# A hybrid decoder trunk on eight cores: attention moved off two PSUM banks, wider masks, a second set of group buffers in the first mixer

## The chip, the cores and the metric

The program runs on all 8 cores of one Trainium2 chip. Each core does one sequence of the batch of 8 alone; nothing is exchanged. The metric is device time in microseconds of the slowest core, the median of several runs. The profile is of one execution, read on its slowest core (core 4).

## The reference

Two layers over x of 8 x 2048 x 1024 (one core: 2048 x 1024). Cut to what matters:

```python
x = x + mamba2_mixer(rms_norm(x, a_norm), ...)        # 8 groups of 4 heads: in_proj, width-4 conv, SSD scan, gated norm, out_proj
x = x + conv_ffn(x, ...)                              # layer 0
k, v = split(rms_norm(x, kv_norm) @ w_kv + b_kv); k = rotary(rms_norm(k, k_norm), positions)
q = rotary(rms_norm(rms_norm(x, b_norm) @ w_q + b_q, q_norm), positions)
x = x + sliding_window_sink_attention(q, k, v, sinks) @ w_o + b_o   # window 128, 16 q heads, 4 kv heads
x = x + conv_ffn(x, ...)                              # layer 1

def sliding_window_sink_attention(q, k, v, sinks):
    # blocks of 128 queries against their own and the previous block of 128 keys
    scores = einsum("bnqhgd,bnkhd->bnhgqk", qb, k_band) * d ** -0.5
    mask = (rel >= 0) & (rel < WINDOW) & (kpos >= 0)
    probs = softmax(concatenate([where(mask, scores, -inf), sink], -1))[..., :-1]
    return einsum("bnhgqk,bnkhd->bnqhgd", probs, v_band)

def conv_ffn(x, norm_g, w_in, conv_w, conv_b, w_down):
    gate, val = split(rms_norm(x, norm_g) @ w_in, [2816])
    return (silu(causal_dwconv(gate, conv_w, conv_b)) * val) @ w_down
```

## The kernel before

The 2048 tokens are cut into four blocks (b = 0 to 3) of 512. The work is written as lists of steps: `mixer_steps(b)`, `mixer_out(b)`, `ffn_steps(b, l)`, `attn_steps(b)`. `weave` merges lists by their costs. In order: mixer 0 alone, its output projection alone; then for b = 0, 1, 2 a stretch with the feed-forward layers beside mixer b + 1, and a stretch with attention of block b beside the output projection of block b + 1; then the last block. In the trace (its page and windows) mixer 0 takes the first 240 us, the three attention stretches lie at about 550 to 650, 1050 to 1155 and 1550 to 1640 us, attention of block 3 lies beside a feed-forward layer near 1800 to 1960 us.

The order in which each engine takes instructions is not that of the lists. Every operation is recorded with a cost and its dependences (`_deps_for`: a PSUM bank is one unit), and `schedule` plays the program: each engine takes the ready operation with the lowest number. So an engine's queue is fixed when the program is built, and at run time a queue stands still when its next instruction waits.

PSUM has 8 banks. Mixers 1 to 3 use banks 0 and 1 for the input projection (`b_in`), 2 for everything small (`b_x`), 3 for the scan's output (`yb`). Their first steps are four norms (transposes `sb_cm,sb_Cs`), then `dt1`: 8 matmuls with 96 output partitions (`sb_hM,sb_ring_mw`, 96x512), a chain of activations and vector operations, and matmuls `sb_cf,sb_Ssb`, `sb_cf,sb_Eb` (`toks`). Attention of blocks 0 to 2 takes its banks from `fh`: projections 1 to 7 in turn, scores the pairs (2,3) and (4,5) in turn, 6 for the output and 7 for the denominators, 1 for `wo` (the output weights, `sb_ring_fw,sb_uF`). The block's output projection (`mixer_out`, `sb_ring_mw,sb_ybuf`) has bank 0 alone. The 34 uses of the projection banks end with `rot(9)` (`sb_fln,sb_cm`, then DVE operations), which falls on bank 6.

Attention is cut into units, one for a pair of kv heads, 128 queries and 128 keys: 14 in block 0, 16 in each other, 62 in all. `qk(u)` issues two 64-row score matmuls (`sb_hF,sb_kT`) and two 32-row matmuls that add the mask as a product of two constants (`sb_cm`); ACT takes the exponential of both banks; `pv(u)` issues two pairs of 64-column matmuls (`sb_facc,sb_vtok` and `sb_facc,sb_cm`). After two units `norm` runs on DVE and ACT before the banks 6 and 7 are free again. Matmuls recorded with `mmg` (line 362 of the profile), `mm` (349) and `tr` (367) carry these names.

A step `yst(t)` of the scan issues two `mmg` groups of four 64-column matmuls. All mixers keep one set of group buffers (`macc`, `Er`, `Eb`, `Wt`, `Cs`, `xtok`, `xE`, `Btok`, `CBb` and others); `fetch(g)` loads `Er` through the SP queue.

## Time and profile before

| | |
|---|---|
| time, median of 3 runs | 2098.79 us (2096.45 to 2115.26) |
| the profiled execution, its own time | 2089.89 us |
| its span on the slowest core (cores: 2070.2 to 2088.8) | 2088.8 us |
| PE busy | 1880.0 us, 90% |
| DVE busy | 1403.8 us, 67% |
| ACT busy | 1328.4 us, 64% |
| chain that ended last | PE 77%, DMA 8%, DVE 5%, ACT 5%, issue 5% |

The span is the time from the first to the last instruction on one core; the device time of that execution is 1.1 us more. TensorE (PE) is busy nine tenths of it, so the question of any change is what it does to the missing tenth, to the clock, and to how closely matmuls follow each other. In the timeline rows the first number is the start, the second how long the piece lasts; a bracket at the end is the idle time before it and who ended it.

### The profile page before, as it was taken

What the parts mean: (1) busy time and instruction counts of PE and PEld (TensorE: products, weight loads), DVE (VectorE), ACT (ScalarE), POOL (GpSimd) and SP (SyncE); (2) the same over time, 40 slices, a digit from 0 to 9 for tenths busy, and PEclk for the clock granted to TensorE, in tenths of its full rate; (3) what the DMA queues carried; (4) which work ended last, traced back from release to release, by engine and by line L of the source; (5) the groups of instructions that cost most, each with busy time, mean ns of one, the idle gap of its engine ahead of it and who ended that gap; (6) DMA issues with size and microseconds to landing.
All of it is one profiled execution on the core that took longest, in us unless ns stands there. A gap on an engine that the chain in (4) does not pass through costs nothing.

```text
span 2088.8 us, 34694 instructions; the slowest of 8 cores (2070.2 to 2088.8 us)
## 1 busy us (share of the span) xinstructions
PE 1880.0 (90%) x10024; PEld 837.9 (40%) x10024; DVE 1403.8 (67%) x2404; ACT 1328.4 (64%) x2238; POOL 203.8 (10%) x325
## 2 busy tenths in 40 slices
PE   4777789998897999999888899999988799999999
PEld 2333344444433444444432444444443344433344
DVE  5687578887745866678674776688675465683462
ACT  4688567978756566666656766677565543675430
POOL 0122101122111011000120000001102000020000
PEclk9999889999899999999999899999989899999999
DMA  8899669898638999845331454644412344333344
GB/s 201 174 213 217 161 148 212 206 220 203 171 102 179 204 220 223 253 141 169 112 121 59 123 162 161 205 151 148 142 61 92 108 154 137 122 131 107 112 154 153
DMA packets 111065, 330.58 MB, mean 158 GB/s; under 512 B 14752, under 2 KB 33312, under 8 KB 110880
## 3 DMA queue, kind: packets, MB, share of 16 engines
q1 hardware_dynamic: 95184, 271.53, 39.9%
q0 software_dynamic: 15696, 56.83, 17.8%
q8 instruction: 86, 1.41, 0.3%
q14 instruction: 99, 0.81, 0.1%
HBM read 318.74 MB, written 66.39 MB: 184 GB/s over the span
## 4 chain that ended last, share of the span: by engine, by line
PE 77%; DMA 8%; DVE 5%; ACT 5%; issue 5%; SPq 0%; DVEq 0%; POOL 0%; ACTq 0%; POOLq 0%
PE ps_ps L349 69%; PE ps_ps L362 6%; DMA sb_ring_mw<-w 3%; PE ps_ps L367 2%; DMA w<-sb_ring_fw 1%; DMA sb_Er<-er_scr 1%; DMA sb_ring_fw<-w 1%; DVE sb_macc L401 1%; ACT sb_facc L385 1%; DVE sb_hF L390 1%; DMA sb_xR<-x 1%; ACT sb_fsq L385 1%; DVE sb_xR L390 0%; ACT L385 0%; ACT sb_Cs L385 0%
## 5 line engine op out<-in xcount | busy, mean ns | idle before, releaser
L349 PE MATMUL ps_ps<-sb_hF,sb_ring_fw 128*128 128x512 bf16 x2464 | 579.9, 385 | 9.9 <-DVE sb_hF L390 6.3
L349 PE MATMUL ps_ps<-sb_hM,sb_ring_mw 128*128 128x512 bf16 (+1 forms) x1568 | 399.8, 394 | 34.7 <-DVE sb_macc L401 25.7
L349 PE MATMUL ps_ps<-sb_ring_fw,sb_uF 128*128 128x512 bf16 (+1 forms) x1696 | 397.8, 381 | 11.2 <-DVE sb_hF L390 3.6
L349 PEld LDWEIGHTS ps_ps<-sb_hF,sb_ring_fw 128*128 128x128 bf16 x2464 | 239.0, 99 | 295.3 <-issue 37.0
L401 DVE SCALAR_TENSOR_TENSOR sb_macc<-ps_ps,sb_cst,sb_macc 128x511 f32<-128x511 f32 (+2 forms) x384 | 282.2, 744 | 12.5 <-PE ps_ps L349 1.4
L385 ACT ACT_TABLE_LOAD x194 | 248.9, 1283 | 43.3 <-PE ps_ps L362 15.5
L401 DVE SCALAR_TENSOR_TENSOR sb_facc<-ps_ps,sb_cst,sb_facc 128x511 f32<-128x511 f32 x352 | 261.6, 745 | 17.5 <-PE ps_ps L349 2.9
L349 PEld LDWEIGHTS ps_ps<-sb_ring_fw,sb_uF 128*128 128x128 bf16 x1696 | 160.5, 99 | 203.4 <-issue 41.6
L349 PEld LDWEIGHTS ps_ps<-sb_hM,sb_ring_mw 128*128 128x128 bf16 (+1 forms) x1568 | 151.3, 101 | 218.7 <-issue 70.6
L385 ACT ACTIVATE sb_facc<-ps_ps,sb_cst 128x512 f32<-128x512 f32 x197 | 150.1, 763 | 135.7 <-PE ps_ps L349 120.0
L390 DVE TENSOR_TENSOR sb_xR<-sb_xR,ps_ps 128x512 f32<-128x512 f32 x128 | 86.8, 685 | 170.3 <-PE ps_ps L349 161.4
L349 PE MATMUL ps_ps<-sb_ring_mw,sb_ybuf 128*128 128x512 bf16 (+1 forms) x608 | 156.3, 389 | 15.4 <-DVE sb_ybuf L401 8.1
L385 ACT ACTIVATE sb_macc<-ps_ps,sb_cst 128x512 f32<-128x512 f32 x135 | 103.8, 769 | 76.0 <-PE ps_ps L349 71.4
L385 ACT ACTIVATE sb_uF<-sb_facc 128x512 bf16<-128x512 f32 x176 | 109.7, 628 | 58.1 <-DVE sb_facc L401 54.4
L390 POOL TENSOR_TENSOR sb_stmp<-sb_prevF,sb_cdec 128x256 f32<-128x256 f32 x128 | 83.9, 655 | 620.0 <-DVE sb_prevF L390 425.5
L390 DVE TENSOR_TENSOR sb_uF<-sb_uF,ps_ps 128x512 bf16<-128x512 bf16 x176 | 119.7, 681 | 31.6 <-PE ps_ps L349 30.2
L385 ACT ACTIVATE sb_prevB<-sb_prevF 128x256 bf16<-128x256 f32 x128 | 52.6, 411 | 74.2 <-PE ps_ps L349 30.8
L390 DVE TENSOR_TENSOR sb_facc<-sb_facc,sb_fix_f 128x2 f32<-128x2 f32 x176 | 29.8, 169 | 97.8 <-ACT sb_halo_f L385 91.3
L349 PEld LDWEIGHTS ps_ps<-sb_ring_mw,sb_ybuf 128*128 128x128 bf16 x608 | 56.5, 100 | 92.1 <-issue 41.9
L390 DVE TENSOR_TENSOR sb_prevF<-sb_stmp,ps_ps 128x256 f32<-128x256 f32 x128 | 53.3, 416 | 54.3 <-PE ps_ps L349 41.1
L401 DVE SCALAR_TENSOR_TENSOR sb_ytmp<-sb_xcb,sb_cst,ps_ps 128x256 f32<-128x256 bf16 x128 | 56.8, 476 | 37.0 <-PE ps_ps L362 36.8
L413 POOL DMA_DIRECT2D sb_ring_fw<-w x76 | 41.8, 550 | 392.4 <-PE ps_ps L349 352.5
(200 smaller groups left out, 2325.6 us busy)
## 6 DMA issues: line engine op xcount, KB each, us to landing
sb_ring_fw<-w SPq DMA_DIRECT2D x218, 512.0 KB, 3.8
sb_ring_mw<-w SPq DMA_DIRECT2D x106, 512.0 KB, 5.0
sb_ring_fw<-w POOLq DMA_DIRECT2D x76, 512.0 KB, 9.6
w<-sb_ring_fw SPq DMA_DIRECT2D x76, 512.0 KB, 8.3
sb_ring_mw<-w POOLq DMA_DIRECT2D x32, 512.0 KB, 9.5
w<-sb_ring_mw SPq DMA_DIRECT2D x32, 512.0 KB, 7.7
sb_Er<-er_scr SPq DMA_DIRECT2D x32, 512.0 KB, 7.6
sb_xR<-x SPq DMA_DIRECT2D x16, 512.0 KB, 9.2
```

Source lines behind the costliest of these rows:

```text
L349: return self.add("pe", lambda e: e.matmul(out, lhsT, rhs, start=start, stop=stop), [lhsT, rhs] + ([] if start else [out]), [out], cost=ma ...
L362: ins = e.matmul(out, lhsT, rhs, start=start, stop=stop)
L367: return self.add("pe", lambda e: e.transpose(out, in_, ident), [in_, ident], [out], cost=250.0 if _f32(in_) else 80.0)
L385: return self.add("act", lambda e: e.activation(out, in_, func, **kw), rd, wr, cost=c, tab=TABLE.get(func, 0))
L390: return self.add(eng, lambda e: e.tensor_tensor(out, in0, in1, op), [in0, in1], [out], cost=c)
L401: return self.add("dve", lambda e: e.scalar_tensor_tensor(out, in0, scalar, in1, op0, op1), rd, [out], cost=190.0 + 1.1 * _n(out))
L413: return self.add(queue, lambda e: e.dma_start(out=out, in_=in_), [in_], [out], dma_sem=sem, cost=900.0 if queue == "pool" else 60.0, lat= ...
```

## The change

Eight things:

- Attention of blocks 0 to 2 keeps to banks 2 to 7: projections over six banks instead of seven, scores in the one pair (2,3) instead of two pairs in turn, `wo` in banks 4 and 5 instead of bank 1. Of the 34 projection uses the last (`rot(9)`) now falls on bank 5.
- `mixer_out` of blocks 1 to 3 takes banks 0 and 1 in turn instead of bank 0.
- Mixers 1 to 3 take banks 0 and 1 for `dt1` and `toks` instead of bank 2, and bank 3 for `dt2`. So `toks` now stands in the turn of the input projection's two banks.
- The mask matmuls contract over 64 rows instead of 32, the rows added being zero in one factor (`mvc`, `mvp`); the constant `cm` grows from 768 to 896 columns.
- `yst` issues its eight matmuls as one group.
- The scheduler knows a mode for groups (1: 64-row, 2: 64-column) and a cost for changing it; a matmul of 512 columns costs 225 ns in it instead of 214.
- In mixer 0, groups 1, 3, 5 and 7 use a second set of buffers, lent by tiles that idle then (`uF`, `facc`, `fsq`, `fln`, `cosT`, `sinT`). So `fetch(1)` is issued beside `fetch(0)`, and each later one a group earlier as far as buffers go.
- At the start `cm` is loaded ahead of x and `cst`.

```diff
 def mmg / schedule
+            elif e == "pe":
+                pick = min(ready[e], key=lambda x: x[0] + (MODE_SWITCH if self.all_ops[x[1]].mode != mode else 0))
...
+            if e == "pe" and op.mode != mode:
+                fin += 100.0
+                mode = op.mode
...
+    K.dma("sp", cm[:], cm_d, "c1")
     xload(0, 0)
     K.dma("sp", cst[:], cst_d, "c0")
-    K.dma("sp", cm[:], cm_d, "c1")
...
+    own = dict(macc=macc[:], Btok=Btok[:], xtok=xtok[:], xE=xE[:], CBb=CBb[:], Er=Er[:], Eb=Eb[:], Wt=Wt[:], Cs=Cs[:],
+               ytmp=ytmp[:], stmp=stmp[:], msq=msq[:], mln=mln[:])
+    lent = dict(macc=facc[:], Eb=uF[:, 0:2, :], Wt=uF[:, 2:6, :], Cs=uF[:, 6:10, :], Er=uF[:, 10:14, :],
+                xtok=flat(uF[:, 14:16, :], 256), xE=flat(uF[:, 16:18, :], 256), CBb=uF[:, 18, :], Btok=flat(uF[:, 19:20, :], 128),
+                ytmp=cosT[:].rearrange("p (a n) -> p a n", n=256), stmp=sinT[:, 0:256], msq=fsq[:], mln=fln[:])
+    def bufs(b, g, *names):
+        s = lent if b == 0 and g % 2 else own
...
-            bk = b_x()
+            bk = b_x() if solo else b_in()
...
-        bo = Banks([0, 1, 2, 3] if solo else [0])
+        bo = Banks([0, 1, 2, 3] if solo else [0, 1])
...
-    fh.proj, fh.sc, fh.o, fh.d, fh.wo = [1, 2, 3, 4, 5, 6, 7], [2, 4], 6, 7, [1]
+    fh.proj, fh.sc, fh.o, fh.d, fh.wo = [2, 3, 4, 5, 6, 7], [2], 6, 7, [4, 5]
...
                     for half in range(2):
-                        o = half * 64 + (32 if prev else 0)
-                        P = slice(o, o + 32)
-                        items.append((sc[half], CMv("mu")[P, :], CMv("mv")[P, :].unsqueeze(1).to_broadcast([32, 4, 128]), False, True))
-                    K.mmg(items, 470.0)
+                        P = slice(half * 64, half * 64 + 64)
+                        items.append((sc[half], CMv("mu")[P, :],
+                                      CMv("mvp" if prev else "mvc")[P, :].unsqueeze(1).to_broadcast([64, 4, 128]), False, True))
+                    K.mmg(items, 450.0, 1)
```

How the order moves. First the PE queue at the end of attention of block 1, where the last `wo` matmuls (`sb_ring_fw,sb_uF`) give way to the feed-forward layer (norm transposes `sb_cm,sb_fsq`, then `sb_hF,sb_ring_fw`). Before:

```order
L367 MATMUL ps_ps<-sb_cm,sb_facc 128x128 x8
L349 MATMUL ps_ps<-sb_ring_fw,sb_uF 128x512 x16
L367 MATMUL ps_ps<-sb_cm,sb_fsq 128x128 x8
L349 MATMUL ps_ps<-sb_hF,sb_ring_fw 128x512 x16
L367 MATMUL ps_ps<-sb_cm,sb_Cs 128x128 x8
L349 MATMUL ps_ps<-sb_hF,sb_ring_fw 128x512 x47
L367 MATMUL ps_ps<-sb_cm,sb_Cs 128x128 x8
L349 MATMUL ps_ps<-sb_hF,sb_ring_fw 128x512 x8
L349 MATMUL ps_ps<-sb_hM,sb_ring_mw 96x512 x8
```

And the same place now:

```order
L352 MATMUL ps_ps<-sb_ring_fw,sb_uF 128x512 x8
L372 MATMUL ps_ps<-sb_cm,sb_Cs 128x128
L352 MATMUL ps_ps<-sb_hM,sb_ring_mw 96x512 x8
L372 MATMUL ps_ps<-sb_cm,sb_fsq 128x128 x8
L352 MATMUL ps_ps<-sb_hM,sb_ring_mw 128x512 x6
L352 MATMUL ps_ps<-sb_hF,sb_ring_fw 128x512 x40
L352 MATMUL ps_ps<-sb_hM,sb_ring_mw 128x512 x2
```

The next mixer's four norms and its `dt1` matmuls now stand ahead of the feed-forward's last norm transposes, and six matmuls of its input projection ahead of the first feed-forward matmul; before, they came after 71 feed-forward matmuls. At the end of attention of block 0 the same stands, with the eight `dt1` matmuls split 2 and 6 about the transposes and none of the input projection.

Second the PE queue where the units of block 1 begin (second score pair, first two `pv`). Before:

```order
L362 MATMUL ps_ps<-sb_hF,sb_kT 128x512 x2
L362 MATMUL ps_ps<-sb_cm 128x512 x2
L362 MATMUL ps_ps<-sb_facc,sb_vtok 64x512 x2
L362 MATMUL ps_ps<-sb_facc,sb_cm 64x512 x2
L362 MATMUL ps_ps<-sb_facc,sb_vtok 64x512 x2
L362 MATMUL ps_ps<-sb_facc,sb_cm 64x512 x2
L349 MATMUL ps_ps<-sb_ring_mw,sb_ybuf 128x512 x3
L362 MATMUL ps_ps<-sb_hF,sb_kT 128x512 x2
```

And now:

```order
L365 MATMUL ps_ps<-sb_hF,sb_kT 128x512 x2
L365 MATMUL ps_ps<-sb_cm 128x512 x2
L365 MATMUL ps_ps<-sb_facc,sb_vtok 64x512 x2
L365 MATMUL ps_ps<-sb_facc,sb_cm 64x512 x2
L352 MATMUL ps_ps<-sb_ring_mw,sb_ybuf 128x512 x3
L365 MATMUL ps_ps<-sb_facc,sb_vtok 64x512 x2
L365 MATMUL ps_ps<-sb_facc,sb_cm 64x512 x2
L352 MATMUL ps_ps<-sb_ring_mw,sb_ybuf 128x512 x6
L365 MATMUL ps_ps<-sb_hF,sb_kT 128x512 x2
```

Six more matmuls of the output projection stand ahead of the third unit's scores, and the first `pv` no longer shares a bank with `rot(9)`. Over the whole PE queue, counted from the two orders, the places where the tile shape changes (full, 64 rows, 32 rows, 64 columns) fall from 637 to 562; 62 of the 75 are the changes from 64 to 32 rows inside a unit. The matmuls are the same 9988.

## Rows read from the trace of the kernel before

**Rows 1.** Windows: mixer 0, the attention stretches, the stretch after the second

```profile
60.00:240.00 180.00, 135.24 (x822) 57.81 (x823) 131.18 (x238) 138.30 (x226) 38.36 (x68) 0.90 0.86 191
565.00:655.00 90.00, 72.86 (x364) 26.84 (x363) 42.58 (x61) 51.29 (x81) 12.48 (x10) 0.89 0.49 125
1075.00:1160.00 85.00, 64.76 (x338) 23.74 (x337) 38.92 (x49) 46.17 (x71) 10.60 (x4) 0.90 0.21 77
1570.00:1650.00 80.00, 61.26 (x304) 21.08 (x302) 37.18 (x46) 40.81 (x62) 10.61 (x4) 0.87 0.26 92
1180.00:1500.00 320.00, 313.28 (x1716) 144.24 (x1714) 247.83 (x450) 220.70 (x372) 21.61 (x43) 0.99 0.50 160
```

**Rows 2.** Timeline of PE in attention of block 1, matmuls close together

```profile
1103.51 1.04 PE L349 MATMUL ps_ps<-sb_ring_fw,sb_uF 128*128 128x512 bf16 x4
1104.47 0.41 PE L362 MATMUL ps_ps<-sb_facc,sb_vtok 128*64 128x512 bf16 x2
1104.71 0.38 PE L362 MATMUL ps_ps<-sb_facc,sb_cm 128*64 128x512 bf16 x2
1105.03 0.39 PE L362 MATMUL ps_ps<-sb_hF,sb_kT 64*128 64x512 bf16 x2
1105.35 0.39 PE L362 MATMUL ps_ps<-sb_cm 32*128 32x512 bf16 x2
1105.67 1.90 PE L349 MATMUL ps_ps<-sb_ring_fw,sb_uF 128*128 128x512 bf16 x8
```

**Rows 3.** Timeline of PE, end of attention of block 1

```profile
1140.89 3.42 PE L349 MATMUL ps_ps<-sb_ring_fw,sb_uF 128*128 128x512 bf16 x8 [1.48 <-DVE sb_hF L390]
1145.26 1.89 PE L349 MATMUL ps_ps<-sb_ring_fw,sb_uF 128*128 128x512 bf16 x8 [0.94 <-DVE sb_xR L390]
1151.25 1.01 PE L367 MATMUL ps_ps<-sb_cm,sb_fsq 128*128 128x128 bf16 x8 [4.10 <-ACT sb_fsq L385]
1153.99 5.42 PE L349 MATMUL ps_ps<-sb_hF,sb_ring_fw 128*128 128x512 bf16 x16 [1.73 <-DVE sb_hF L390]
```

**Rows 4.** Timeline of PE, first units of block 1

```profile
1082.58 0.39 PE L362 MATMUL ps_ps<-sb_cm 32*128 32x512 bf16 x2
1088.07 0.64 PE L362 MATMUL ps_ps<-sb_facc,sb_vtok 128*64 128x512 bf16 x2 [5.10 <-DVE sb_facc L390]
...
1089.92 1.46 PE L349 MATMUL ps_ps<-sb_ring_mw,sb_ybuf 128*128 128x512 bf16 x3
1091.31 0.61 PE L362 MATMUL ps_ps<-sb_hF,sb_kT 64*128 64x512 bf16 x2
```

**Rows 5.** Timeline of DVE there

```profile
1082.02 2.56 DVE L390 TENSOR_TENSOR sb_uF<-sb_fln,sb_cosT 128x512 f32<-128x512 bf16 x1
1084.50 2.82 DVE L390 TENSOR_TENSOR sb_hF<-sb_uF 128x512 bf16<-128x512 f32 x1
1087.24 0.68 DVE L390 TENSOR_TENSOR sb_facc<-ps_ps,sb_sinT 128x512 f32<-128x512 f32 x1
...
1088.44 1.64 DVE L390 TENSOR_TENSOR sb_hF<-sb_uF,sb_facc 128x512 bf16<-128x512 f32 x1
```

**Rows 6.** Timeline of POOL there

```profile
1081.69 10.60 POOL L390 TENSOR_TENSOR sb_xR<-sb_xR,sb_uF 128x1024 f32<-128x1024 f32 x4 [42.93 <-ACT sb_facc L385]
```

**Rows 7.** Who PE waited for, 1075 to 1160 us: us, times, longest

```profile
PE ps_ps L367 <- ACT sb_fsq L385: 4.1, 1, 4.1
...
PE ps_ps L349 <- DVE sb_xR L390: 2.4, 3, 0.9
PE ps_ps L362 <- DVE sb_uF L390: 2.4, 3, 1.4
```

**Rows 8.** Groups by line and shape: exponentials of the scores, blocks 0 to 2

```profile
L385 ACT ACTIVATE sb_facc<-ps_ps 128x1024 bf16<-128x1024 f32 x46 | 46.6, 1020 | 45.8 <-PE ps_ps L362 45.7
```

**Rows 9.** Who PE waited for in mixer 0, 14 to 235 us

```profile
PE ps_ps L349 <- DVE sb_macc L401: 14.0, 11, 2.6
...
PE ps_ps L362 <- DMA sb_SL<-as_scr: 3.9, 1, 3.9
```

More of the change, by code:

```diff
@@ L327, in add @@
         op.prio = None
+        op.mode = 0
         op.eng = eng
@@ L349, in mm, with mmg @@
         return self.add("pe", lambda e: e.matmul(out, lhsT, rhs, start=start, stop=stop),
[L350 to L352 removed]
+                        [lhsT, rhs] + ([] if start else [out]), [out], cost=max(70.0, 0.44 * _n(out)))
+    def mmg(self, items, cost, mode):
         rd, wr = [], []
@@ L431, in schedule @@
         table = 0
+        mode = 0
         def key(op):
```

47 lines of the change are left out of this document (28 added, 19 removed).

## The prediction

> **What bounds the kernel now.** I read the page first: PE is busy 90% of the span and carries 77% of the chain that ended last, DVE and ACT stand at 67% and 64%. So time is won where PE stands still, where its clock is low, or where matmuls follow each other less closely. The windows [rows 1] say where. In the 320 us after the second attention stretch PE is busy 313 us at a granted clock of 0.99: nothing but fewer or closer matmuls helps there. In the three attention stretches it is busy 72.86 of 90, 64.76 of 85 and 61.26 of 80 us, at clocks of 0.89, 0.90 and 0.87: 17, 20 and 19 us idle, 56 us in all. In mixer 0 (180 us shown) it is busy 135 us, but there DVE is busy 131, ACT 138, and the DMA share is 0.86. Then the timeline inside attention: matmuls of one tile shape, a change of shape [rows 2], the end of the stretch [rows 3], its first units [rows 4 to 6], and the list of waits [rows 7].
>
> **The change part by part.**
>
> *Masks of 64 rows.* Between the two pairs of 64-column matmuls 0.24 us pass (1104.47 to 1104.71); from such a pair to the 64-row scores 0.32, and from the scores to the 32-row masks 0.32 again [rows 2]. Full matmuls follow each other at (1.90 - 1.04) / 4 = 0.215 us [rows 2]. A pair of half-height matmuls runs side by side in the time of one, so a change of tile shape costs 0.32 - 0.215 = 0.10 us. With masks of 64 rows the change inside each unit goes: 62 x 0.10 = 6.5 us of PE. The counted order has 13 changes fewer besides, 1.4 us. About a fifth of the units stand next to a wait that would swallow this, so I take 6 us, bounds 3 and 8. The Trainium skill (TensorEngine Tiling (Array Packing), Key Properties) says that a change of tiling mode drains TensorE, and TensorE: Matmul & The Clock Gate (Single matmul latency) puts such a drain near 175 ns; as an estimate by these pages the 75 changes would give 13 us instead of 8. The trace shows 0.10 us, and the measurement decides.
>
> *The end of attention.* In block 1 PE waits 1.48, 0.94, 4.10 and 1.73 us in 15 us [rows 3], the longest for the activation of the last norm. In the new order the next mixer's norms, its 8 `dt1` matmuls and up to 6 of its input projection stand ahead of the feed-forward's first matmul. 8 to 14 matmuls at 0.215 us are 1.7 to 3.0 us, and about twice that at the clock of this place: 8 `wo` matmuls take 3.42 us, a later 8 take 1.89 [rows 3], which is the 1.2 GHz level against 2.4, the first 8 after 1.48 us in which PE stood still: the 4.10 us can be filled, and since that work comes out of a stretch that is PE-bound [rows 1], what is filled is won. `wo` in two banks removes the 0.94 us, which is a wait for the bank to be added into xR. A part stays: 1.48 and 1.73 us are waits for DVE that the moved work stands behind or beside. The low clock itself costs (3.42 - 1.89) for 8 matmuls and 5.42 - (15 x 0.215 + 0.38) = 1.8 for 16, 3.3 us; if PE has work in the gap some of it goes. I take 5 us each for blocks 0 and 1: 10 us, bounds 2 (the norms' extra work on ACT makes the feed-forward's norm late and only `wo` gains) and 2 x (4.10 + 0.94 + 3.3) = 17. After block 2 there is no mixer: only the 0.94 us wait goes, counted below.
>
> *The first units.* The first `pv` waits 5.10 us [rows 4]. It is ready to run but for bank 6, whose last user is `rot(9)`: it starts when the DVE operation at 1087.24 is over [rows 5]. DVE is late because two of its operations last 2.56 and 2.82 us where such an operation on 512 columns takes 0.68, inside the 10.60 us in which POOL adds the bias to xR [rows 5, 6]. With `rot(9)` on bank 5 the `pv` of units 0 and 1 and six more output matmuls stand ahead of the wait, but the third unit's scores still need the query that `rot(9)` writes, at 1088.44 + 1.64 = 1090.1 [rows 5]. So the wait does not go, it moves behind 4 x 0.215 + 6 x 0.215 = 2.2 us of work. With a little of the clock (the first `pv` pair takes 0.64 us instead of 0.41 [rows 2, 4]) I take 2.5 us each for blocks 1 and 2, at whose starts this wait stands: 5 us, bounds 0 and 10.
>
> *Two banks for the output projection.* PE waits for DVE's addition into xR 2.4 us in this stretch, three times [rows 7], one of them the 0.94 above. I take 0.8 us per block beyond it, and 0.9 us for block 2's `wo`: 3 us, bounds 0 and 5.
>
> *One pair of score banks.* This adds a wait. `qk(u+1)` may start only when ACT has read the scores of `qk(u)`. The exponential lasts 1.02 us and there are 46 in blocks 0 to 2 [rows 8]. What is queued behind a waiting `qk` is all of PE: the `pv`, `wo` and output projection matmuls. Before, such a wait had another pair of banks as cover. From the first `pv` at 1088 [rows 4] to the last `wo` at 1141 [rows 3] a unit has 53 / 16 = 3.3 us, and its scores, the exponential and two hand-overs need about 0.54 + 1.02 + 0.2 = 1.8; the new order puts 3 to 9 other matmuls between a unit's scores and the next. So mostly nothing; where ACT is inside a norm (an activation of 1024 columns is about 1 us) the scores come late. Cost 3 us, bounds 0 and 46 x 1.02 = 47 us (every wait open).
>
> *Mixer 0 with a second set of buffers.* PE waits 14.0 us for DVE's conv operations, which hold its PSUM banks [rows 9]; other SBUF buffers do not free those. What the second set removes is that the next group's masks and weights wait for the last `yst` of this one. But DVE and ACT are busy 73% and 77%, and DMA 86% of the stretch [rows 1]: if DMA ran without a pause the 180 us would be 155, and nothing of the loads goes. I take 4 us, bounds -3 (a second `Er` transfer now goes ahead of the small `SL` rows, for which PE already waits 3.9 us [rows 9]) and 13. `cm` first: PE has its identity earlier, but the last x tile lands after nearly the same bytes; nothing.
>
> *`toks` in the input projection's banks.* In mixers 1 to 3 a chain of activations and vector work must end before the second bank is free, where before three input projections ran ahead. Feed-forward matmuls are there to fill PE (busy 98% of the window after attention [rows 1]); nothing, bounds 0 and 3 us lost.
>
> *Sum.* 6 + 10 + 5 + 3 - 3 + 4 = 25 us, against the profiled execution's 2089.89 us: 2065. The median of the shown runs is 8.9 us above that execution. Set against the median, and taking 2 us off since not all of this will come together, 2098.8 - 23 = **2076 us**.
>
> **The rivals.**
>
> *The gaps move but don't close.* Filling the end of attention may only push the same waits on: the norm of the feed-forward and the mixer's norms and `dt1` chain share ACT and DVE, and the mixer that starts earlier is woven to the same place in the PE queue. For it: in the first units the wait demonstrably only moves. Against it: work done in a gap is missing later from a stretch that is 98% busy. It would leave the masks, 6, and the two banks, 3: -9 us, 2090.
>
> *Everything comes.* Clock and gaps recover fully and mixer 0 comes near its DMA bound: 8 + 17 + 10 + 5 + 10 - 2 = 48 us, 2051. Against it: all upper bounds at once.
>
> *Single score banks bind (slower).* One mechanism: each `qk` stands at the head of PE's queue until its predecessor's exponential is done, and ACT gets to it late, being busy over half of the stretch (51.29 of 90 us [rows 1]) with norms in a fixed order. Price: up to 1.02 us for each of 46 units, 47 us, against the 25 + 3 = 28 us of the other terms: 2099 + 19 = 2118. It decides from 28 / 46 = 0.6 us of wait per unit. For it: PE waited 2.4 us for the norm chain [rows 7] already with four score banks. Against it: a unit has 3.3 us and needs 1.8.
>
> *The change doesn't do what it says.* The next mixer may not begin beside attention: its matmuls may sit in the queue behind waits for its own norms. This is the first rival's number.
>
> **How the numbers follow.** The forecast, gains of some 15 to 32 us (2067 to 2084): 0.50. Gaps only move, 2084 to 2098: 0.25. Everything comes, 2045 to 2067: 0.13. Score banks bind, 2098 to 2125: 0.12. The range leaves out less than half of each outer case: 2052 to 2104. Faster by over 1% means below 2077.8, about what a measurement of this kernel can tell from no change: half of the first case and more, 0.37, and the third, 0.13, make 0.50; slower by over 1% (above 2119.8) is the end of the last, 0.06; the rest 0.44.
>
> **What the profile of the changed kernel would show.** Masks: score and mask pairs 0.22 us apart instead of 0.32. End of attention: between the last `wo` and the first feed-forward matmul, `dt1` matmuls and no wait above 2 us; in the waits, the 4.1 us for `sb_fsq` gone or under 1. First units: no wait for `sb_facc` before `pv`, in its place one of about 3 us for DVE before the third scores. Two banks: waits for `sb_xR` near zero. Score banks: new waits of PE for ACT `sb_facc`, in sum under 5 us; above 15 the slower rival is right. Mixer 0: its output projection begins some 4 us earlier. The prediction is wrong if new waits for DVE or ACT appear in the 98% busy stretches, or if the clock in the attention stretches stays at 0.89 with less work left after them.

## The result and the profile after

The changed kernel takes 2032.12 us (median of 4 runs, 2029.83 to 2036.23) where the kernel before takes 2097.62 (4 runs). The ratio is 0.9678 with the interval 0.9615 to 0.974: about 67 us won. The forecast was 2076 and its range ended at 2052: the direction was right, the size a third of what came. In some executions of either kernel the cores of one die show a lower clock and take longer; all ratios here leave those out. The profiled execution has spans of 2007.6 to 2029.1 us on the eight cores and a granted clock of 0.971 to 0.979 (before 0.952 to 0.960).

First the page of the kernel after: busy time, share and instructions of each engine.

```profile
PE 1850.7 (91%) x10024; PEld 823.7 (41%) x10024; DVE 1405.7 (69%) x2404; ACT 1319.1 (65%) x2232; POOL 207.9 (10%) x325
```

Then its windows, shifted to where the same work now lies, against [rows 1] (columns: stretch, length, busy us of PE, its weight load, DVE, ACT, POOL, granted clock, DMA share, GB/s):

```profile
56.00:236.00 180.00, 139.58 (x852) 59.79 (x851) 139.61 (x250) 146.60 (x239) 40.71 (x69) 0.92 0.88 191
545.00:635.00 90.00, 78.50 (x412) 29.43 (x410) 52.45 (x77) 60.72 (x99) 13.23 (x12) 0.92 0.58 144
1052.00:1137.00 85.00, 74.36 (x417) 29.18 (x414) 53.53 (x78) 56.42 (x97) 11.05 (x4) 0.96 0.29 93
1530.00:1610.00 80.00, 70.04 (x371) 25.91 (x370) 45.79 (x64) 50.42 (x81) 10.62 (x4) 0.96 0.28 100
1150.00:1470.00 320.00, 313.26 (x1733) 143.02 (x1732) 238.95 (x431) 215.30 (x362) 23.06 (x45) 1.00 0.49 159
```

The dense stretch (last row) is as busy as before. In the three attention stretches PE is busy 6 to 10 us more and its clock is 0.92 to 0.96 where it was 0.87 to 0.90; they hold 371 to 417 matmuls instead of 304 to 364.

Where the time went, by stage. I cut every core's PE timeline at the first feed-forward matmul (`sb_hF,sb_ring_fw`), at the first and last scores (`sb_kT`) of each block and at the next feed-forward matmul, and take the median over the eight cores, so the columns need not add up exactly. "Idle" is what PE's rows leave uncovered. "Dense 1" and "dense 2" are the stretches from the end of attention of block 0 (1) to the first scores of block 1 (2).

| stage | before, us (idle) | after, us (idle) | won |
|---|---|---|---|
| mixer 0 and its output projection | 268.0 (78.9) | 261.8 (73.8) | 6.2 |
| feed-forward beside mixer 1 | 305.3 (19.6) | 296.5 (16.5) | 8.8 |
| units of block 0 | 45.6 (4.4) | 43.6 (2.0) | 2.0 |
| end of block 0 | 26.0 (11.7) | 18.5 (6.1) | 7.5 |
| dense 1 | 428.8 (21.3) | 425.2 (21.7) | 3.6 |
| units of block 1 | 49.5 (7.4) | 47.5 (4.4) | 2.0 |
| end of block 1 | 26.1 (12.0) | 18.2 (5.9) | 7.9 |
| dense 2 | 419.8 (14.2) | 411.5 (14.0) | 8.3 |
| units of block 2 | 47.4 (6.1) | 49.3 (6.6) | -1.9 |
| end of block 2 | 28.2 (12.2) | 9.5 (3.3) | 18.7 |
| up to block 3's units | 224.0 (10.6) | 221.7 (12.4) | 2.3 |
| block 3's units | 80.7 (0.1) | 77.8 (0.7) | 2.9 |
| tail | 131.0 (4.1) | 132.8 (4.2) | -1.8 |

Idle time falls from 202.6 to 171.5 us, 31 us. The other half is the same matmuls taking less time: 29 us by PE's busy time on the two pages (1880.0 and 1850.7), 36 us if all of the 67 that is not idle time is put there. The 75 fewer changes of tile shape at 0.10 us would be 7.5 of it. The rest goes with the clock, whose median over the cores rises from 0.954 to 0.975; how much of it that is was not separated.

The largest single stage is one to which the forecast gave only 0.9 us. Its timeline on PE in the kernel before (start, us, engine, line, operation; in brackets the idle time ahead and who ended it):

```profile
1632.59 1.04 PE L349 MATMUL ps_ps<-sb_ring_fw,sb_uF 128*128 128x512 bf16 x4
1635.91 1.86 PE L349 MATMUL ps_ps<-sb_ring_fw,sb_uF 128*128 128x512 bf16 x4 [2.28 <-DVE sb_uF L390]
1638.71 3.57 PE L349 MATMUL ps_ps<-sb_ring_fw,sb_uF 128*128 128x512 bf16 x8 [0.94 <-DVE sb_xR L390]
1643.22 0.61 PE L367 MATMUL ps_ps<-sb_cm,sb_fsq 128*128 128x128 bf16 x8 [0.94 <-DVE sb_xR L390]
1647.14 1.01 PE L367 MATMUL ps_ps<-sb_cm,sb_fsq 128*128 128x128 bf16 x8 [3.31 <-ACT sb_fsq L385]
1649.75 1.86 PE L349 MATMUL ps_ps<-sb_hF,sb_ring_fw 128*128 128x512 bf16 x4 [1.59 <-DVE sb_hF L390]
```

and the same place in the kernel after:

```profile
1585.58 0.41 PE L365 MATMUL ps_ps<-sb_facc,sb_vtok 128*64 128x512 bf16 x2 [1.43 <-DVE sb_uF L395]
...
1586.57 1.90 PE L352 MATMUL ps_ps<-sb_ring_fw,sb_uF 128*128 128x512 bf16 x8
1588.31 0.61 PE L372 MATMUL ps_ps<-sb_cm,sb_facc 128*128 128x128 bf16 x8
1588.75 0.61 PE L372 MATMUL ps_ps<-sb_cm,sb_fsq 128*128 128x128 bf16 x8
1589.89 1.89 PE L352 MATMUL ps_ps<-sb_ring_fw,sb_uF 128*128 128x512 bf16 x8 [0.52 <-DVE sb_uF L395]
1593.10 2.10 PE L352 MATMUL ps_ps<-sb_hF,sb_ring_fw 128*128 128x512 bf16 x9 [1.32 <-DVE sb_hF L395]
```

Before, two norms (`sb_cm,sb_fsq`) stand one behind the other after the last `wo`, at a clock that makes 8 `wo` matmuls last 3.57 us; 9 us of waiting stand in these rows. After, the norms' transposes run ahead of the last `wo`, which takes 1.89 us, and 1.84 us of waiting is left from there.

The end of attention of block 1, against [rows 3]:

```profile
1112.17 1.89 PE L352 MATMUL ps_ps<-sb_ring_fw,sb_uF 128*128 128x512 bf16 x8
1113.90 0.22 PE L372 MATMUL ps_ps<-sb_cm,sb_Cs 128*128 128x128 bf16 x1
1116.14 1.90 PE L352 MATMUL ps_ps<-sb_hM,sb_ring_mw 128*96 128x512 bf16 x8 [2.02 <-DVE sb_hM L395]
1118.17 0.61 PE L372 MATMUL ps_ps<-sb_cm,sb_fsq 128*128 128x128 bf16 x8
1118.96 1.46 PE L352 MATMUL ps_ps<-sb_hM,sb_ring_mw 128*128 128x512 bf16 x6 [0.19 <-ACT sb_Eb L390]
1120.36 1.89 PE L352 MATMUL ps_ps<-sb_hF,sb_ring_fw 128*128 128x512 bf16 x8
```

The last 8 `wo` matmuls, the 8 of `dt1`, 6 of the input projection and the feed-forward's first run at full clock with one wait of 2 us between them; 4.10 and 1.73 us are gone.

The first units of block 1, PE, against [rows 4]:

```profile
1054.61 0.39 PE L365 MATMUL ps_ps<-sb_hF,sb_kT 64*128 64x512 bf16 x2
1054.82 0.39 PE L365 MATMUL ps_ps<-sb_cm 64*128 64x512 bf16 x2
...
1057.24 0.41 PE L365 MATMUL ps_ps<-sb_facc,sb_vtok 128*64 128x512 bf16 x2
...
1059.14 1.47 PE L352 MATMUL ps_ps<-sb_ring_mw,sb_ybuf 128*128 128x512 bf16 x6
1064.47 0.61 PE L365 MATMUL ps_ps<-sb_hF,sb_kT 64*128 64x512 bf16 x2 [3.86 <-DVE sb_hF L395]
1064.84 0.66 PE L365 MATMUL ps_ps<-sb_cm 64*128 64x512 bf16 x2
```

The `pv` waits no more; the third unit's scores wait 3.86 us instead. Scores and masks are 0.21 us apart (1054.61 to 1054.82) where they were 0.32 [rows 2].

Last, whom PE waited for in mixer 0, against [rows 9] (us, times, longest):

```profile
PE ps_ps L352 <- DVE sb_macc L406: 6.7, 8, 1.9
...
PE ps_ps L352 <- DVE sb_facc L406: 4.9, 6, 1.6
...
PE ps_ps L365 <- DMA sb_SL<-as_scr: 2.2, 1, 2.2
```

In the kernel after, the odd groups of mixer 0 have their conv accumulator in `facc`, so the wait for conv is the sum of the first two rows, 11.6 us against 14.0.

### The profile page after: what moved, and what is told of

Its sections match the earlier page's. It is cut to its first block, busy times and chain, and to the rows that moved or that the text cites. A ratio compares the mean times of both kernels' runs of the same rounds, so it can differ in the third digit from the quotient of the medians.

```text
span 2029.1 us, 34704 instructions; the slowest of 8 cores (2007.6 to 2029.1 us)
## 1 busy us (share of the span) xinstructions
PE 1850.7 (91%) x10024; PEld 823.7 (41%) x10024; DVE 1405.7 (69%) x2404; ACT 1319.1 (65%) x2232; POOL 207.9 (10%) x325
## 3 DMA queue, kind: packets, MB, share of 16 engines
q0 software_dynamic: 15696, 56.83, 18.5%
## 4 chain that ended last, share of the span: by engine, by line
PE 76%; DMA 7%; issue 6%; DVE 6%; ACT 5%; SPq 0%; POOL 0%; DVEq 0%; ACTq 0%; POOLq 0%
PE ps_ps L352 68%; PE ps_ps L365 5%; DMA sb_ring_mw<-w 2%; DMA sb_ring_fw<-w 2%; PE ps_ps L372 2%; DMA w<-sb_ring_fw 1%; DMA w<-sb_ring_mw 1%; ACT sb_facc L390 1%; DVE sb_hF L395 1%; DVE sb_facc L406 1%; DVE sb_macc L406 1%; ACT L390 1%; DMA sb_xR<-x 1%; ACT sb_macc L390 0%; DVE sb_xR L395 0%
## 5 line engine op out<-in xcount | busy, mean ns | idle before, releaser
L406 DVE SCALAR_TENSOR_TENSOR sb_facc<-ps_ps,sb_cst,sb_facc 128x510 f32<-128x510 f32 (+2 forms) x400 | 296.6, 745 | 20.3 <-PE ps_ps L352 2.1
L406 DVE SCALAR_TENSOR_TENSOR sb_macc<-ps_ps,sb_cst,sb_macc 128x511 f32<-128x511 f32 x336 | 248.9, 745 | 15.9 <-DVE sb_macc L406 0.5
L390 ACT ACTIVATE sb_facc<-ps_ps,sb_cst 128x512 f32<-128x512 f32 x213 | 162.5, 764 | 120.3 <-PE ps_ps L352 109.9
L395 POOL TENSOR_TENSOR sb_stmp<-sb_prevF,sb_cdec 128x256 f32<-128x256 f32 x112 | 76.4, 682 | 572.2 <-DVE sb_prevF L395 421.5
L390 ACT ACTIVATE sb_macc<-ps_ps,sb_cst 128x512 f32<-128x512 f32 x119 | 91.3, 768 | 65.5 <-PE ps_ps L352 58.4
L395 DVE TENSOR_TENSOR sb_prevF<-sb_stmp,ps_ps 128x256 f32<-128x256 f32 x112 | 46.7, 417 | 49.0 <-PE ps_ps L352 45.4
L352 PE MATMUL ps_ps<-sb_hM,sb_ring_fw 128*128 128x512 bf16 x352 | 78.8, 388 | 1.6 <-DVE sb_hM L395 1.6
```

The source lines that it names most:

```text
L352: return self.add("pe", lambda e: e.matmul(out, lhsT, rhs, start=start, stop=stop), [lhsT, rhs] + ([] if start else [out]), [out], cost=ma ...
L390: return self.add("act", lambda e: e.activation(out, in_, func, **kw), rd, wr, cost=c, tab=TABLE.get(func, 0))
L395: return self.add(eng, lambda e: e.tensor_tensor(out, in0, in1, op), [in0, in1], [out], cost=c)
L406: return self.add("dve", lambda e: e.scalar_tensor_tensor(out, in0, scalar, in1, op0, op1), rd, [out], cost=190.0 + 1.1 * _n(out))
```

## The experiments

All ratios are to the kernel before. To compare them I turn each into microseconds won of 2097.6 (so the kernel after has won 67.5). Intervals are some 0.002 to 0.009 on either side. Two of them together make a difference between two variants uncertain by 10 to 20 us, so a difference of that size is taken here as real only where the single times lie apart or the stages show it. The single executions of the kernel after took 2029.8 to 2036.2 us; "single times" below are the same for a variant. The stages, where named, are medians over the cores, cut as above; they come from one execution each.

**Bank 1 and the next norms.** The feed-forward layer behind block 2 is the first of block 3 and rotates its norms over all eight banks (`ids`, `ffn_steps`), the second one falling on bank 1, which `wo` held. Undone in the kernel before by the order of the list alone:

```diff
-            ids = list(range(8)) if b == NBLK - 1 else [4, 5, 6, 7]
+            ids = [2, 3, 4, 5, 6, 7, 0, 1] if b == NBLK - 1 else [4, 5, 6, 7]
```

> The kernel before with one edit: the feed-forward layers of the last block take their banks in the turn 2 to 7, 0, 1 instead of 0 to 7, so its four norm transposes stand in banks 2 to 5 and none in bank 1, in which the output weights of attention of block 2 work. Theory A (the 18.7 us that the end of the third attention stretch gained come from bank 1 being shared by those matmuls and the next block's norms): the stretch from the last scores of block 2 to the first feed-forward matmul, 28.2 us before, falls to 15 to 22 us and the time by 6 to 13 us, ratio 0.994 to 0.997. Theory B (one bank for the output weights is too few, whoever shares it): it stays within 2 us of 28.2 and the time within 0.2%.

Measured 0.9913 (0.987 to 0.9955), 18 us won. By stage only the end of block 2 moves, 28.2 to 14.8 us, all others within 2.2. Its timeline:

```profile
1629.28 0.61 PE L367 MATMUL ps_ps<-sb_cm,sb_facc 128*128 128x128 bf16 x8 [0.70 <-ACT sb_facc L385]
1630.84 0.61 PE L367 MATMUL ps_ps<-sb_cm,sb_fsq 128*128 128x128 bf16 x8 [0.95 <-ACT sb_fsq L385]
1632.15 1.02 PE L349 MATMUL ps_ps<-sb_ring_fw,sb_uF 128*128 128x512 bf16 x4 [0.71 <-DVE sb_uF L390]
1633.39 1.02 PE L349 MATMUL ps_ps<-sb_hF,sb_ring_fw 128*128 128x512 bf16 x4 [0.22 <-DVE sb_hF L390]
1634.25 1.89 PE L349 MATMUL ps_ps<-sb_ring_fw,sb_uF 128*128 128x512 bf16 x8
```

The feed-forward's matmuls now stand between the last `wo`s, and no wait in these rows reaches 1 us. `wo` still has one bank here, so the shared bank was the cause: 13 us by the stages, more than half of that stage's 18.7.

**One `wo` bank.** The kernel after with `fh.wo = [5]`.

```diff
-    fh.proj, fh.sc, fh.o, fh.d, fh.wo = [2, 3, 4, 5, 6, 7], [2], 6, 7, [4, 5]
+    fh.proj, fh.sc, fh.o, fh.d, fh.wo = [2, 3, 4, 5, 6, 7], [2], 6, 7, [5]
```

> The changed kernel with one edit: the output weights of attention of blocks 0 to 2 have bank 5 alone instead of banks 4 and 5. Theory A (sharing of bank 1 with the next block's norms): the ends of the three stretches (last scores to first feed-forward matmul, 18.5, 18.2 and 9.5 us in the changed kernel) grow by at most 3 us each, the time by under 8 us over the changed kernel (ratio to before 0.968 to 0.972). Theory B (one bank is too few): they go back to some 25, 25 and 25 us, 25 to 30 us in sum, ratio 0.980 to 0.983.

Measured 0.9799 (0.9759 to 0.9839): 42 us won, so the second bank is worth 25 (single times 2052.7 to 2055.8, clear of the kernel after). The ends of blocks 0 and 1 go back to 26.7 and 22.8 us (18.5 and 18.2 in the kernel after); the end of block 2 does not (6.3); 4.5 us more go in dense 1, 4.5 up to block 3's units and 3.2 in the units of block 1. So the two ends that the next mixer stands behind need two `wo` banks, and the third needs a bank that its successor does not want.

**Attention's banks alone.** The kernel before with the line of the kernel after:

```diff
-    fh.proj, fh.sc, fh.o, fh.d, fh.wo = [1, 2, 3, 4, 5, 6, 7], [2, 4], 6, 7, [1]
+    fh.proj, fh.sc, fh.o, fh.d, fh.wo = [2, 3, 4, 5, 6, 7], [2], 6, 7, [4, 5]
```

> The kernel before with the attention banks alone (projections 2 to 7, scores in the pair 2,3, output weights in 4 and 5); the output projection keeps bank 0, dt1 and toks bank 2, masks, planner and buffers as before. If the bank of the output weights is the cause of what was missed, most of the gain is here: 25 to 35 us less, ratio 0.983 to 0.988. If the planner's new costs or the closer matmuls are: under 12 us, ratio over 0.994. If single score banks bind: slower than before.

Measured 0.9883 (0.9836 to 0.993), 24.5 us won. The ends give 8.2, 1.1 and 16.7 us and dense 2 gives 19; but the feed-forward beside mixer 1 loses 7.6 and the units of the three blocks 3.1, 4.9 and 5.8. The units hold 22, 28 and 21 matmuls more than before, about 5 us each at 0.215, so it is mostly work moved in from dense 2; their idle time rises by 2.9 us in all. One pair of score banks can have cost no more than a part of that: over the whole kernel PE's score matmuls wait 2.2 us for an exponential (0.3 before), median over the cores. In the kernel after it is less still:

```profile
PE ps_ps L365 <- ACT sb_facc L390: 0.6, 2, 0.3
```

That the end of block 1 gives only 1.1 us here, with two `wo` banks, shows that the second bank needs the right order around it.

**All bank edits.** The same and the rest of them in the kernel before (`dt1` and `toks` in `b_in()`, `dt2` in bank 3):

```diff
-        bo = Banks([0, 1, 2, 3] if solo else [0])
+        bo = Banks([0, 1, 2, 3] if solo else [0, 1])
...
-            bk = b_x()
+            bk = b_x() if solo else b_in()
```

> The kernel before with every bank edit of the change and nothing else: attention on banks 2 to 7, one pair of score banks, wo on 4 and 5, the output projection on 0 and 1, dt1 and toks of mixers 1 to 3 in the input projection's banks, dt2 in the y bank. Masks of 32 rows, planner costs and the single set of group buffers stay. It gains over the run with the attention's banks alone (2073) what the output projection's second bank and the mixer's freedom from bank 2 bring. Theory (banks carry most of the gain, by the block ends): end of attention of blocks 0, 1, 2 at or under 18, 20, 11 us against 26, 26, 28, total 2058 (2050 to 2064); what then stays to 2032 is masks, planner and buffers, some 25 us. Rival 1 (the banks are everything and the other edits worth nothing together): 2032 to 2042. Rival 2 (the mixer's own bank edits and the second output bank are worth nothing): 2072, as with the attention's banks alone.

Measured 0.9891 (0.9844 to 0.9937), 23 us won: near rival 2's number, though the ends are at 17.9, 18.9 and 10.5 us, as short as after. The ends and dense 2 win 50 us; the feed-forward beside mixer 1 (+7.4), the units (+1.1, +8.5, +6.7), mixer 0 (+2.8) and dense 1 (+2.3) give 29 back. Whom PE waited for in the units of block 1:

```profile
PE ps_ps L349 <- DVE sb_xR L390: 4.5, 1, 4.5
PE ps_ps L362 <- DVE sb_uF L390: 2.8, 2, 2.1
PE ps_ps L367 <- ACT sb_facc L385: 0.9, 1, 0.9
```

So banks explain the ends but not the total, and my theory that they carry most of it fell here.

**The mixer's banks.** The kernel after with `dt1`, `toks` and `dt2` back on bank 2 (`bk = b_x()`, three places).

> The kernel after with dt1, toks and dt2 of mixers 1 to 3 back in bank 2, which attention's scores and projections hold. The next mixer's dt matmuls then cannot start until the last exponential has read bank 2, and all its later dt work waits for the block end. Theory (the next mixer's start beside attention is worth little, two wo banks and free norm banks fill the block ends): end of attention stays near 18 us in blocks 0 and 1, total 2034 to 2038. Rival (the start beside attention is what fills them, as the forecast put it): 22 to 25 us at both ends, 2042 to 2048.

Measured 0.9685 (0.9662 to 0.9708), 1.5 us from the kernel after, ends of 17.5 and 19.4 us. The mixer's start beside attention, to which the forecast gave the filling of the gap, does not need these banks; this part is worth nothing that can be measured in the kernel after.

**The planner's numbers out of the kernel after.**

```diff
-MODE_SWITCH = 10
+MODE_SWITCH = 0
...
-                fin += 100.0
+                fin += 0.0
...
-cost=max(70.0, 0.44 * _n(out))
+cost=max(70.0, 0.418 * _n(out))
```

> The kernel after with the planner's numbers of before (no charge for a change of tile shape, 0.418 instead of 0.44 ns a column). The counted order has 576 changes of tile shape instead of 562, 14 more. Theory (the planner is worth its changes and no more): 14 x 0.10 = 1.4 us, 2034 (2030 to 2038). Rival (the planner's costs put the work into better places, which is the part of the gain that no bank explains): 2045 or more, the loss spread over the dense stretches (426 and 413 us in the kernel after).

Measured 0.9808 (0.9757 to 0.9859): 27 us of the 67.5 go with them (single times 2054.4 to 2062.6). The feed-forward beside mixer 1 takes 306.4 us instead of 296.5, mixer 0 266.2 instead of 261.8, dense 1 432.4 instead of 425.2, the units of block 1 54.1 instead of 47.5 (idle 9.8 instead of 4.4); dense 2 wins 9. Its order has 576 changes of shape against 562, which is 1.4 us.

**The planner's numbers alone**, in the kernel before (the lines of the change for `mmg` and `schedule`, with 0.44 ns a column):

> The kernel before with the planner's new numbers alone (0.44 ns a column, the charge for a change of tile shape); banks, masks, buffers as before. Its order has 612 changes instead of 637: 2.5 us. Theory (the planner's numbers pay where one pair of score banks leaves no slack: with four score banks they bring little): 2097 - 2.5 - a little = 2090 to 2096. Rival (they bring their 25 us whatever the banks): 2072.

Measured 1.0000 (0.9977 to 1.0024). The ends of blocks 1 and 2 are 3.6 and 4.9 us shorter and the units of blocks 1 and 2 too, mixer 0 is 4.7 longer, the next stage 4.8, dense 1 7.2. Alone they are worth nothing that can be measured (5 us either way).

**Banks and planner together**, masks and buffers as before:

> The kernel before with all bank edits and the planner's new numbers; masks of 32 rows and one set of group buffers stay. Banks alone gave 2074 (0.9891), the planner alone 2097 (1.0000). Theory (the two need each other: the planner's new numbers take back what the banks' new order loses, up to the output projection of mixer 1 and in the units): 2055 or less, near 2097 - 66 + 14 (buffers) + 7 (masks) = 2052. Rival 1 (they add up, banks 23 and planner 0; masks and buffers together are then worth 40): 2070 to 2076. Rival 2 (the effect of the planner's numbers on the time is that of any other shuffle of the order, and needs all the parts to be as they are): anything from 2055 to 2080, with the stage to the first feed-forward matmul and the next one moving by 5 to 10 us each without a wait of their own.

Measured 0.9815 (0.978 to 0.9849), 39 us: 16 more than banks (23) and planner (0) alone add up to. The units of blocks 1 and 2 go from 58.0 and 54.1 us to 47.9 and 47.8, the feed-forward beside mixer 1 from 312.7 to 307.1; dense 2 gives 9 of it back. In the units of block 1 one wait is left:

```profile
PE ps_ps L364 <- DVE sb_hF L394: 4.0, 1, 4.0
```

The two act together: with the changed banks the old plan leaves matmuls behind DVE's additions and norms in the units of block 1, the new one does not. The rival that the planner's numbers merely reshuffle the order and this shuffle fell well (2055 to 2080) is not excluded by the number, 2058.

**Which of the planner's numbers.** The kernel after with 0.418 ns a column and the charge kept; then with 0.44 and the charge at zero (the two halves of the diff above).

> The kernel after with one number changed: the planner takes 0.418 instead of 0.44 ns per matmul column; its charge for a change of tile shape stays. The order has 559 changes of tile shape (562 in the kernel after). With both planner numbers undone the time was 2057, 25 us above the kernel after, of which the 14 changes pay 1.4. Theory (the number sets when the planner thinks that PE's results and buffers are there, and 0.44 is nearer to the truth, since the kernel's 10340 matmuls take more time than 0.418 a column with changes and clock): most of the 25 us returns with it, 2048 to 2056, with waits of PE in the units of block 1 (4.4 us idle in the kernel after, 9.8 with both undone). Rival (the charge for the tile shape is what counts): 2034.

> The kernel after without the planner's charge for a change of tile shape (neither the 10 that sway the choice nor the 100 ns added to the time); 0.44 ns a column stays. The order has 580 changes of tile shape instead of 562: 18 x 0.10 = 1.8 us. Theory (the charge is worth its changes, the column cost the rest): 2034 to 2040. Rival (the 100 ns for each of 562 changes, 56 us of planned time, are what brings the plan near to the chip): 2048 to 2056, idle time of PE in block 1's units back at 9 us.

Measured 0.9757 (0.9736 to 0.9778) and 0.9796 (0.9732 to 0.9861): 17 and 25 us lost against 27 for both; the intervals do not tell the three apart. Taking out either loses most of what the pair is worth, so their effects do not add up, and neither is the cause by itself. What is in common is another order of the PE queue. In both, most of the loss lies in mixer 0 and the stage behind it (15.6 and 21.4 us by the stages), and for the first in dense 1 (6.5).

**Masks.** The kernel before with the 64-row masks, and the kernel after with the 32-row ones (the mask lines of the change, one way and the other).

> The kernel before with the masks of 64 rows alone. As predicted, 62 changes of tile shape go at 0.10 us: 6 us less, ratio 0.997, and score and mask pairs stand 0.22 us apart instead of 0.32. Rival (the masks are most of what the prediction missed, because in the attention stretches PE's clock recovers when the pairs stand closer): 15 us or more, ratio under 0.993 and a granted clock above 0.93 in the attention stretches.

> The kernel after with the low-rank masks on 32 rows for each half again, a change of tile shape inside each of the 62 units. Theory (the price of the changes, as in the kernel before, where the 64-row masks alone gained 0.0047, 10 us): 6.5 to 10 us more, 2038 to 2042. Rival (beside one pair of score banks a shorter unit only waits longer for the exponential): under 4 us, 2036.

Measured 0.9953 (0.993 to 0.9976) and 0.9727 (0.969 to 0.9763). The first is 10 us won, between 5 and 15; the forecast was 6, bounds 3 and 8. The second would be 10 us lost, but that is not clear of noise: the single times, 2033.7, 2034.9 and 2042.6 us, overlap those of the kernel after, and by the stages the units of all four blocks lose 3.0 us where the first kernel's win 7.8. In both pairs the order of the PE queue is the same with either mask, so these are the cleanest pairs here: the time that PE's rows cover, median over the cores, falls by 4.6 us in the one and rises by 4.1 in the other.

**Group buffers.**

```diff
-        s = lent if b == 0 and g % 2 else own
+        s = own
```

> The kernel after with one set of group buffers in mixer 0. Theory (as predicted, small): mixer 0 to the first feed-forward matmul is 266.2 us in the kernel after and 270.1 before, so it goes back by 4, total 2036 (2032 to 2040). Rival 1 (the second set is worth more than the stage shows, since PE waits for the conv results 9.8 us in the whole kernel instead of 26.2): 10 to 16 us lost, 2042 to 2048. Rival 2 (bound by the loads, nothing is lost): 2032, first stage 266.

Measured 0.9745 (0.9712 to 0.9779), 14 us lost, the number of rival 1 (single times 2041.6 to 2049.2). Its reason does not hold: it counts the conv wait of the kernel after in `macc` alone. With `facc` that wait is 12.5 us in mixer 0 and its output projection, against 14.4 with one set (medians over the cores); after the first 20 us all of PE's waits there fall from 62.7 to 55.7. What falls most is the wait for the scan's state (`prevF`), 9.2 to 5.2, and for `ybuf`, 8.5 to 3.9. The order of the PE queue changes as well. The stage of mixer 0 is 271.9 us instead of 261.8, the next one 300.3 instead of 296.5, dense 1 429.4 instead of 425.2. In the kernel before, that stage reads 268.0, so the difference of the two kernels there (6.2) hides a part of what the buffers bring: the other edits cost mixer 0 some 4 us (within its spread over the cores, 265 to 275 us).

**The wait that moved, taken at its source.** The four additions of the output bias into x on POOL wait for the last exponential issued before the first `norm`, instead of running when the bias has landed.

```diff
-                for t in range(4):
-                    K.tt(x[:, t, :], x[:, t, :], bob, OP.add, eng="pool")
...
+            def addx():
+                for t in range(4):
+                    o = K.tt(x[:, t, :], x[:, t, :], bob, OP.add, eng="pool")
+                    o.deps.append(cur["exp"])
+                cur["exp"].signal = True
...
+                    if last and pi == 1 and nl == 0:
+                        S.append((0.0, addx))
```

> The kernel after, with the four additions of the output bias into x on POOL (10.60 us each block) held back until the exponentials of the first units of a block have been done. In the kernel after PE still waits 3.86 us for the query of the third unit at the start of block 1, with two DVE operations of 2.56 and 2.82 us beside these additions in the kernel before. Theory (a DVE operation beside a POOL operation is slowed four-fold, and that is the wait): those DVE operations take 0.7 us, the wait goes in blocks 1 and 2, 3 to 4 us each, total 2025 (2022 to 2028). Rival 1 (the DVE operations are long for a reason of their own, or the next DVE step is as late): their times and the total stay, 2032. Rival 2 (the additions meet the DVE work of the later units, the y norms and the output additions there, and the wait moves): DVE operations of 2.5 us further on, 2032 to 2038.

> The kernel after with the four bias additions of POOL held back behind the first exponentials, a second time and with more rounds, since the first had few undisturbed executions (2013 to 2025). Theory (a slowed DVE was the wait at the first units): 0.962 to 0.963 of the kernel before, 2017 to 2020, 12 to 15 us below the kernel after. Rival (the first three executions were lucky cores): 0.966 or more, 2026 and up.

Measured 0.9622 (0.9579 to 0.9665), and in the second run 0.9608 (0.9572 to 0.9644), 2010.65 us. That is 0.007 or 15 us below the kernel after; the single times of the second run are 2003.4 to 2023.0. The order of PE's matmuls is the same as in the kernel after, so no reshuffle is behind it. DVE at the first units of block 1, first in the kernel after:

```profile
1055.95 0.68 DVE L395 TENSOR_TENSOR sb_uF<-ps_ps,sb_sinT 128x512 f32<-128x512 f32 x1
1056.56 2.25 DVE L395 TENSOR_TENSOR sb_uF<-sb_fln,sb_cosT 128x512 f32<-128x512 bf16 x1
1058.73 2.83 DVE L395 TENSOR_TENSOR sb_hF<-sb_uF 128x512 bf16<-128x512 f32 x1
1061.49 0.68 DVE L395 TENSOR_TENSOR sb_facc<-ps_ps,sb_sinT 128x512 f32<-128x512 f32 x1
1062.09 0.67 DVE L395 TENSOR_TENSOR sb_xR<-sb_xR,ps_ps 128x512 f32<-128x512 f32 x1
1062.68 1.64 DVE L395 TENSOR_TENSOR sb_hF<-sb_uF,sb_facc 128x512 bf16<-128x512 f32 x1
```

with POOL beside it:

```profile
1055.48 11.05 POOL L395 TENSOR_TENSOR sb_xR<-sb_xR,sb_uF 128x1024 f32<-128x1024 f32 x4 [38.69 <-DMA sb_uF<-bo]
```

then DVE with the late additions (second run):

```profile
1054.65 0.68 DVE L395 TENSOR_TENSOR sb_uF<-ps_ps,sb_sinT 128x512 f32<-128x512 f32 x1
1055.25 0.68 DVE L395 TENSOR_TENSOR sb_uF<-sb_fln,sb_cosT 128x512 f32<-128x512 bf16 x1
1055.85 0.69 DVE L395 TENSOR_TENSOR sb_hF<-sb_uF 128x512 bf16<-128x512 f32 x1
1056.45 0.68 DVE L395 TENSOR_TENSOR sb_facc<-ps_ps,sb_sinT 128x512 f32<-128x512 f32 x1
```

where POOL starts later:

```profile
1065.99 9.30 POOL L395 TENSOR_TENSOR sb_xR<-sb_xR,sb_uF 128x1024 f32<-128x1024 f32 x4 [51.63 <-ACT sb_facc L390]
```

and PE's first `pv` and third scores, with no wait ahead of them:

```profile
1056.46 0.41 PE L365 MATMUL ps_ps<-sb_facc,sb_vtok 128*64 128x512 bf16 x2
...
1058.35 1.47 PE L352 MATMUL ps_ps<-sb_ring_mw,sb_ybuf 128*128 128x512 bf16 x6
1059.75 0.39 PE L365 MATMUL ps_ps<-sb_hF,sb_kT 64*128 64x512 bf16 x2
```

The same two operations take 0.68 and 0.69 us instead of 2.25 and 2.83, and the wait is gone, not moved: units of blocks 1 and 2 fall to 42.0 and 43.4 us (47.5, 49.3), and the stretch up to block 3's units to 214.9 (221.7), where the same additions stand. That is 18 us in three stages.

**Is 0.44 a true cost or a lucky order?** The kernel with the late additions and 0.46, 0.43 and 0.45 ns a column, otherwise the same.

> The kernel with the late bias additions, and 0.46 ns a column in the planner instead of 0.44. Theory (0.44 is a value by which this order happens to come out well, and the planner's costs are a lottery of some 10 us): 2025 to 2040 against 2018. Rival (the nearer the planned time is to the chip's, the better; matmuls of 512 columns follow each other at 0.215 us, 0.42 ns a column, and PE is busy 0.44 ns a column and more with its clock): no more than 3 us from 2018.

> Late bias additions, 0.43 ns a column in the planner; at 0.44 this kernel takes 0.9608 of the kernel before, at 0.46 it takes 0.9734, and at 0.418, with the early additions, the loss was 17 us. Theory (each value gives another order, and how an order falls is luck): somewhere from 0.960 to 0.975, not between its neighbours by size. Rival (a smooth best value near 0.44): 0.960 to 0.965, 2012 to 2022.

> Late bias additions, 0.45 ns a column in the planner. Theory (luck of an order): from 0.960 to 0.975. Rival (a smooth best value near 0.44): between 0.9608 and 0.9734, near 0.965 to 0.968.

Measured 0.9734 (0.969 to 0.9779) at 0.46; 0.9599 (0.9517 to 0.9682) at 0.43; 0.9611 (0.9526 to 0.9696) at 0.45; 0.9608 at 0.44. The three lower values, 0.43 to 0.45, cannot be told apart, and the scatter that I expected did not come. The time is worse at 0.46 (26 us over 0.44's), with the late additions, and at 0.418 (17 us), with the early ones. The loss at 0.46 has no place of its own: 7 us in dense 1, 4 each in mixer 0 and the next stage, 3 in dense 2, and idle time up by 14 us. So the question stays open: 0.44 is no single lucky value, but that it is a truer cost is not shown either, since full matmuls follow each other at 0.215 us [rows 2], which is 0.42 ns a column.

## Why the prediction was wrong, by its steps

*The step that failed first* is "After block 2 there is no mixer: only the 0.94 us wait goes". It looked for what could fill the gap and found nothing; it did not ask whose bank the next norm would take. That norm's turn was bank 1, and the edit of `fh.wo` freed it: 28.2 to 9.5 us in that stage where 0.9 was forecast. The list reordered by itself gives 13 of them, shown by the first experiment. The gap was not to be filled, it was self-made.

*The planner* was priced by the 13 changes of shape fewer, 1.4 us, and nothing for its column cost. With the new banks both together are worth 16 us (masks and buffers as before) to 27 (out of the kernel after), though nothing in the old kernel. This is the second failed step: a cost in the planner was taken for a count of what it avoids, while it moves the whole order. By which moves the stages up to mixer 1 gain is not settled: the losses there appear as short waits and clock, on no one instruction.

*Mixer 0*: 4 us forecast, bounds -3 and 13; its removal costs 14. "DMA share 0.86: nothing of the loads goes" spoke against a gain, but the share rose to 0.88 and PE's busy time with it, 135 to 140 us in 180. This term was mis-sized, by 10 us. The mechanism (the next group's masks and weights need not wait for this one's last `yst`) was not tried by itself: PE waits less for `prevF` and `ybuf`, but for the buffers that are doubled (`Wt`, `Eb`, `xtok` and the like under either name) 8.3 us against 7.8, so how the second set brings its gain stays open. The prediction was right that a second set does not free the PSUM banks from conv: 14.4 us of that wait become 12.5. It was right, too, that `cm` first brings nothing: `dt1` of mixer 0 starts at 24.3 us where it started at 23.9 (medians over the cores).

*Masks*: 6 forecast, 10 measured in the kernel before, with 6 inside the interval. The 0.10 us for each change is right by the spacing (0.21 us apart now). All changes that the masks take away, fully paid (637 to 572 in the order with the masks alone, 65), give 6.5 us. Whether there is more to it than the spacing the runs do not tell.

*End of attention*: 5 us each forecast for blocks 0 and 1; 7.5 and 7.9 measured by stage. The picture was right (norms, `dt1` and 6 matmuls of the input projection ahead of the feed-forward, full clock, no long wait), the reason half so: two `wo` banks are needed (one costs 25 us in all), while the mixer's own banks can be left out of the kernel after. The banks are not enough by themselves: with attention's alone block 1's end gave 1.1 us.

*First units*: the wait went where it was said to go, 3.86 us before the third scores against the "about 3" named. The gain by stage is 2.0 and -1.9 us, but 22 and 21 matmuls more run inside. Its cause, POOL beside DVE, was named too, and is shown by the late additions.

*Single score banks*: cost 3 us forecast; the scores' waits for exponentials come to 0.6 us in the kernel after. One pair was not tried without the other banks, but the slower rival is ruled out. *Two banks for the output projection*: the waits for `sb_xR` are gone in the window of block 1, and over the whole kernel they fall from 6.0 to 1.5 us (medians over the cores); the part was not tried alone, and with the mixer's banks it adds nothing to attention's (23 against 24.5 us). *The merged `yst`* was not tried.

The parts in the order in which they were stacked: all banks 23; planner 16; masks, merged `yst` and `cm` first 15; buffers 14; together 67.5. Each is a difference of two ratios and uncertain by 10 us or more, and another order of stacking would give other shares. Against that the forecast's terms are 15 for the banks, 0 for the planner, 6 for the masks and 4 for the buffers: by these figures it missed the planner's 16 whole, 10 of the buffers, 9 of the masks' group and 8 of the banks. "Everything comes" was 2051 because its bounds were the bounds of my own terms, and two parts had none: the end of block 2 beyond 0.9 us, and the planner.

## What to carry to other kernels

Before a bank is moved, list for each stage border whose turn it is on that bank on the other side; a rotation that begins on a bank still in use can cost more (13 us here) than the banks inside the stage. A change of a planner's cost is a change of the whole order: do not price it by its own count, and give it a term with both signs, since it was worth 0 alone and 16 to 27 us beside new banks. When a change lends a second buffer, add up the waits under both names before saying that a wait has gone. When a wait is going to move and not to go, look at what makes its releaser late: POOL's additions, moved back by some 11 us where they met DVE's work, were worth 15 us of the whole.
